# Value products of the plain, dilated and sparse heads in two column halves, with the probabilities weighted ahead

## The reference

```python
def hybrid_mixer(x, w_in, sinks, lam_p, sub_g, w_out, layer_idx, cos, sin):
    proj = jnp.einsum('bld,dk->blk', x, w_in)
    ...
    acc, m, l = banded_attention(qa, ka, va, SWA_WINDOW - 1)        # A: 8 heads, 2 key/value heads, a sink
    oa = (acc * (corr / den)[..., None]).reshape(b, A_HEADS, L, HEAD_DIM)
    ...
    ob = diff_attention(...)                                        # B: 4 heads, values 128 wide
    ob = ob * lax.rsqrt(jnp.mean(jnp.square(ob), -1, keepdims=True) + RMS_EPS) * sub_g * (1.0 - lam_init)
    oc = dilated_mixture(...)                                       # C: 8 heads
    od = dsa_attention(...)                                         # D: 8 heads, one value head, keys chosen
    mixed = jnp.concatenate([merge(oa), merge(ob), merge(oc), merge(od)], -1).astype(x.dtype)
    return jnp.einsum('blk,kd->bld', mixed, w_out)

def peer_ffn(x, wq, sub_keys, u, v):
    ...
        h = jnp.einsum('td,tkd->tk', xt, u[et])
        a = gt * jax.nn.gelu(h, approximate=False)
        return jnp.einsum('tk,tkd->td', a.astype(v.dtype), v[et])
```

## Time and profile before

| | us |
|---|---|
| median of 3 runs | 3949.77 (3948.16 to 3950.01) |
| the profiled execution's own time | 3949.41 |
| its span | 3947.6 |
| PE busy | 3889.0 (99%) |
| DVE busy | 2638.2 (67%) |
| ACT busy | 1980.8 (50%) |

### The profile page before, as it was taken

One profiled execution on the slowest core, in us unless ns is written; L12 is line 12 of the kernel. 1 busy time (PEld: TensorE's weight loads), 2 busy tenths in 40 slices (PEclk: granted clock), 3 DMA queues, 4 the chain that ended last, 5 costly groups with the idle time before them and its releaser, 6 DMA issues.

```text
span 3947.6 us, 63698 instructions
## 1 busy us (share of the span) xinstructions
PE 3889.0 (99%) x20356; PEld 3313.9 (84%) x20356; DVE 2638.2 (67%) x5016; ACT 1980.8 (50%) x2840; POOL 507.6 (13%) x716
## 2 busy tenths in 40 slices
PE   8999999999999999999999999999999999999998
PEld 6888888888898888888778878888888988888886
DVE  6765688658865555555677555886588655555556
ACT  4564545654565444444455544456555654444443
POOL 1100000730072000000011000017201710000000
PEclk9999999999999999999999999999999999999999
DMA  5435556559645666666644354654695456666664
GB/s 213 160 139 203 176 192 212 177 188 289 216 170 192 239 229 228 227 228 228 233 160 153 136 203 172 211 209 173 201 284 204 173 212 229 227 228 228 229 231 172
DMA packets 244174, 806.66 MB, mean 204 GB/s; under 512 B 24928, under 2 KB 157536, under 8 KB 159328
## 3 DMA queue, kind: packets, MB, share of 16 engines
q1 hardware_dynamic: 207200, 771.65, 56.2%
q10 hardware_dynamic: 36864, 33.57, 2.5%
HBM read 752.69 MB, written 52.43 MB: 204 GB/s over the span
## 4 chain that ended last, share of the span: by engine, by line
PE 96%; DVE 2%; ACT 1%; POOL 0%; DMA 0%; issue 0%; SPq 0%; ACTq 0%; DVEq 0%; POOLq 0%
PE bank L463 27%; PE bank L465 14%; PE bank L681 12%; PE bank L682 12%; PE bank L683 12%; PE bank L477 5%; PE bank L479 5%; PE bank L478 5%; PE bank L643 3%; PE bank L525 1%; PE bank L505 1%; PE bank L518 1%; PE bank L450 0%; DMA iota_k<-iota 0%; PE bank L620 0%; PE bank L490 0%
## 5 line engine op out<-in xcount | busy, mean ns | idle before, releaser
L1070 DVE TENSOR_TENSOR lo<-raw,hi 128x1024 fp32r<-128x1024 f32 x1312 | 1615.0, 1231 | 1015.0 <-ACT hi L730 967.8
L730 ACT ACTIVATE hi<-raw 128x1024 fp32r<-128x1024 f32 x1312 | 1388.6, 1059 | 1496.2 <-PE bank L683 756.9
L463 PE MATMUL bank<-xhl,hi 128*128 128x512 f32 x4608 | 1201.1, 396 | 3.6 <-DVE xhl L1086 2.2
L463 PEld LDWEIGHTS bank<-xhl,hi 128*128 128x128 f32 x4608 | 814.1, 189 | 136.8 <-DVE xhl L1086 2.8
L681 PE MATMUL bank<-hi,xhl 128*128 128x512 f32 x2048 | 797.8, 390 | 7.1 <-DVE xhl L1514 4.4
L682 PE MATMUL bank<-lo,xhl 128*128 128x512 f32 x2048 | 797.4, 389 | 0.0
L683 PE MATMUL bank<-hi,xhl 128*128 128x512 f32 x2048 | 797.2, 389 | 0.0
L465 PEld LDWEIGHTS bank<-xhl,lo 128*128 128x128 f32 x4608 | 655.7, 190 | 64.4
L465 PE MATMUL bank<-xhl,lo 128*128 128x256 f32 x4608 | 672.0, 282 | 0.0
L681 PEld LDWEIGHTS bank<-hi,xhl 128*128 128x128 f32 x2048 | 384.7, 188 | 88.1 <-DVE lo L1070 5.2
L683 PEld LDWEIGHTS bank<-hi,xhl 128*128 128x128 f32 x2048 | 384.9, 188 | 79.9
(11 more groups left out here) (149 smaller groups left out, 2229.3 us busy)
## 6 DMA issues: line engine op xcount, KB each, us to landing
raw<-u_t SPq DMA_DIRECT2D x256, 1024.0 KB, 5.0
raw<-v_t SPq DMA_DIRECT2D x256, 1024.0 KB, 4.8
raw<-w_in SPq DMA_DIRECT2D x80, 1024.0 KB, 4.8
raw<-w_out SPq DMA_DIRECT2D x32, 1024.0 KB, 4.8
raw<-wq SPq DMA_DIRECT2D x32, 1024.0 KB, 4.8
gelu_scratch<-gelu_out ACTq DMA_DIRECT2D x256, 128.0 KB, 3.1
scr<-gelu_scratch SPq DMA_DIRECT2D x256, 128.0 KB, 4.6
gates_scratch<-arena SPq DMA_DIRECT2D x32, 512.0 KB, 9.7
```

The costliest lines, as they stand in the source:

```text
L463: pe.matmul(acc[:], w, xhl[:, c, :, :].rearrange("p a t -> p (a t)"), start=(c == 0), stop=False)
L730: act.activation(hi[j % NSPLIT][:], half, ACT.Copy).then_inc(hi_done, 1)
L1070: dve.tensor_tensor(lo[j % NSPLIT][:], half, hi[j % NSPLIT][:].bitcast(F32), ALU.subtract).then_inc(lo_done, 1)
```

## The change

The value products of the heads of A, C and D are done for two heads at a time, in `pair_values`: now 64 columns of values are stationary and the 128 columns of the transposed probabilities are moving. The result of the first head goes to partitions 0 to 63 of the bank, that of the second to 64 to 127, so the result is already transposed (head elements on partitions, tokens along the row) and needs no turn of `mixed`. As the row sums would then lie along the row, the probabilities are divided ahead: ACT multiplies them by the inverted sums (`weigh`, two instructions for a head, in the slot after the exponentials), and `turn_probs` waits for that. `take_out` becomes a plain copy for A and D and nothing for C, whose result ACT and DVE split straight from the bank. Only the four heads of B still go through `mixed_b` and two turns (k = 4 and 5). Two more edits come with it: the wait for `iota_in` on DVE moves from the kernel's start to just before the expert selection, and the last products of each layer take, for token block 0, the half tiles one after another over all banks.

```diff
-    out = {t + 2: (e[0], e[1]) for t, e in slots.items() if e[0] in ("A", "D")}
+    out = {t + 2: (e[0], e[1] // 2) for t, e in slots.items() if e[0] in ("A", "D") and e[1] % 2}
@@ tensor
                     def turn_step(r, src, k):
-                        if r == 1 and k < 2:
-                            pe.wait_ge(v_stored, NB)
-                        elif r == 1 and k < 4:
+                        if r == 1:
                             pe.wait_ge(masked_done, NB * N_HEAD_ITEMS)
-                        elif r == 1:
-                            pe.wait_ge(turn_lo, n - 1)
+                            pe.wait_ge(rms_scaled, 4 * (k - 3))
...
-                            pe.wait_ge(exp_done, NB * (head_item(n) + 1))
+                            pe.wait_ge(weighted, NB * (WEIGHTED_NO[kind, h] + 1))
...
+                    def pair_values(dst, srcs, at):
+                        for b in range(NB):
+                            for kb in range(b + 1):
+                                for i in range(2):
+                                    last = pe.matmul(dst[i * HD:(i + 1) * HD, b * P:(b + 1) * P], vals[:, kb, at[i]:at[i] + HD],
+                                                     srcs[i][:, (b + kb) * P:(b + kb + 1) * P], start=(kb == 0), stop=(kb == b))
...
-                            for i in range(4):
-                                last = head_values(bank[7 - h][:, i * 2 * HD:(i + 1) * 2 * HD], probs_t_c[4 * h + i],
-                                                   V_C + HD * (4 * h + i), HD)
+                            for i in range(2):
+                                c = 4 * h + 2 * i
+                                last = pair_values(bank[7 - h][:, i * L:(i + 1) * L], probs_t_c[c:c + 2], [V_C + HD * c, V_C + HD * (c + 1)])
...
-                            last = head_values(bank[7], probs_t[j % 2], V_A + HD * (h // 4) if kind == "A" else V_D, HD)
+                            at = V_A + HD * (h // 2) if kind == "A" else V_D
+                            last = pair_values(bank[7], probs_t[2 * (j % 2):2 * (j % 2) + 2], [at, at])
...
-                        if t in MIXED_TURN_AT:
-                            turn_step(1, mixed, MIXED_TURN_AT.index(t))
+                        if t in MIXED_TURN_AT and MIXED_TURN_AT.index(t) in (4, 5):
+                            turn_step(1, mixed_b, MIXED_TURN_AT.index(t))
...
-                    for q in range(D // W):
-                        for j in (BODY - 4 + q // 2, BODY - 2 + q // 2):
-                            pe.wait_ge(lo_done, N_HALVES - BODY + j + 1)
-                            pe.wait_ge(al_done, NT - NRAW + j // 2 + 1)
-                            last = products(0, j, j // 2 % 2, stop=j >= BODY - 2, qs=(q % 2,))
-                        last.then_inc(y_done, 1)
+                    for j in range(BODY - 4, BODY):
+                        pe.wait_ge(lo_done, N_HALVES - BODY + j + 1)
+                        pe.wait_ge(al_done, NT - NRAW + j // 2 + 1)
+                        for q in range(2):
+                            last = products(0, j, j // 2 % 2, stop=j >= BODY - 2, qs=(q,))
+                            if j >= BODY - 2:
+                                last.then_inc(y_done, 1)
@@ scalar
+                        if r == 1 and k < 4:
+                            act.wait_ge(head_out, 2 * k + 2)
+                            act.wait_ge(half_used, AT_IN + N_IN - HPG + k + 1)
+                            act.activation(xh[:, 2 * k:2 * k + 2, :], mixed_t[:, 2 * k:2 * k + 2, :], ACT.Copy).then_inc(turn_hi, 1)
+                            return
...
+                    def weigh(n):
+                        kind, h, part = ITEMS[n]
+                        if kind == "B":
+                            return
+                        act.wait_ge(summed_up, WEIGHTED_NO[kind, h] + 1)
+                        for b in range(NB):
+                            i = NB * head_item(n) + b
+                            cols = pm[n % 4][:, block_cols[b]]
+                            act.activation(cols, cols, ACT.Identity, scale=st[:, 2, i:i + 1]).then_inc(weighted, 1)
...
+                        for n in ITEM_AT.get(t - 1, ()):
+                            if n >= N_INDEX:
+                                weigh(n)
@@ vector
                         dve.wait_ge(prepared, 4)
-                        dve.wait_ge(iota_in, 16)
...
+                        dve.tensor_copy(mixed_t[:, h + (4 if kind == "D" else 0), :], bank[7][:, 0:L]).then_inc(head_out, 1)
...
+                    dve.wait_ge(iota_in, 16)
                     for b in range(NB):
                         with dve.Fori(0, PH) as h:
```

More of the change, by code:

```diff
@@ L134, in build @@
     VALUE_AT, VALUE_NO = value_events()
-    N_SHORT = 2 * 8
+    N_TAKEN = 4 + 4 + len(B_VALUES_AT)
+    WEIGHTED_NO = {(kind, h): n for n, (kind, h, part) in enumerate(i for i in ITEMS if i[0] in ("A", "D", "C"))}
     ITEM_NO = {item: n for n, item in enumerate(ITEMS)}
@@ L191, in build @@
         ln2_gb, _ = region(16 * L, 2, D)
-        mixed, at = region(at, NB, D)
+        mixed_t, at = region(at, 8, L)
+        mixed_b, at = region(at, NB, W)
         bias_causal, at = region(at, L)
@@ L215, in build @@
         sel_flat = sel.rearrange("p a b n -> p (a b n)")
+        probs_t = [at[:, i * HEAD_COLS:(i + 1) * HEAD_COLS] for at in (scr[:, 1536:2304], sel_flat) for i in range(2)]
         probs_t_c = ([arena[:, h * HEAD_COLS:(h + 1) * HEAD_COLS] for h in range(2)]
@@ L254, in turn_bank @@
             if r == 1:
-                return bank[k] if k < 2 else bank[4 + k % 2]
+                return bank[13 - k] if k >= 6 else bank[4 + k % 2]
             return bank[4 + k % 4]
@@ L272, in build @@
         irelu, iacc = sem("irelu"), sem("iacc")
+        summed_up, weighted = sem("summed_up"), sem("weighted")
         scored, masked_done = sem("scored"), sem("masked_done")
@@ L447, in turn_step @@
                             pe.wait_ge(normed_dve, (2 if r and layer else 0) + k // 4 + 1)
+                        first_c = 8 if r == 1 else 0
                         for c in (2 * k, 2 * k + 1):
@@ L527, in head_values @@
                         return last
+                    def pair_values(dst, srcs, at):
[4 more added lines that the diff above has]
+                                                     srcs[i][:, (b + kb) * P:(b + kb + 1) * P], start=(kb == 0), stop=(kb == b))
+                        return last
                     def values(kind, h):
@@ L732, in turn_high @@
                     def turn_high(r, k):
-                        act.wait_ge(turned, r * (DC // 2) + k + 1)
+                        if r == 1 and k < 4:
[3 more added lines that the diff above has]
+                            return
+                        if r == 1 and k >= 6:
+                            act.wait_ge(pv_done, VALUE_NO["C", k - 6] + 1)
+                        else:
+                            act.wait_ge(turned, {0: k + 1, 1: DC // 2 + k - 3, 2: DC // 2 + 2 + k + 1}[r])
                         if r == 1:
@@ L1075, in turn_low @@
                         full = turn_bank(r, k)
-                        if r != 1 and k % 2 == 0:
+                        if r == 1 and k < 4:
+                            full = mixed_t[:, two, :].rearrange("p a b -> p (a b)")
+                        elif r != 1 and k % 2 == 0:
                             full = turn_f[0]
@@ L1322, in rms_scale @@
                             h, b = j // 2, j % 2
-                            cols = mixed[:, b, MIX_B + 2 * HD * h:MIX_B + 2 * HD * (h + 1)]
+                            cols = mixed_b[:, b, 2 * HD * h:2 * HD * (h + 1)]
                             dve.scalar_tensor_tensor(out=cols, in0=cols, scalar=small[:, 40 + j:41 + j], in1=subg_b, op0=ALU.mult,
```

45 lines of the change are left out of this document (13 added, 32 removed).

## The result

| | us |
|---|---|
| changed kernel, median of 6 runs | 3923.39 (3922.21 to 3924.08) |
| kernel before, median of 6 runs beside it | 3949.89 (3947.26 to 3950.64) |
| ratio | 0.9934, 95% interval 0.9922 to 0.9945 |
| profiled execution after: its own time, its span | 3923.11, 3921.3 |
| forecast | 3927, range 3920 to 3942 |

A forecast was written before the change was run, and what follows sets the result against it. PE, busy 3889.0 of 3947.6 us, was taken as the bound. Gains of 5.3 (turns), 8.2 (value products), 7.5 (start) and 1.7 (between layers) sum to 22.7 us: 3927 us, range 3920 to 3942.

The forecast's parts named there:

- What bounds the kernel: Whole kernel: PE is busy 3889.0 of 3947.6 us, so nearly every product removed from PE shortens it.
- Mixed turns: PE's turns of `mixed`: six go in each of two layers at 0.44 us each, 5.3 us gained.
- Value products: Value products of A, D and C in two column halves, two at a time: 8.2 us gained, bounds 14.2 and -7.6.
- The rival of one half after the other: Value products: column halves don't overlap, only 6.9 us gained in all, 3943 us; chance 16%.
- Weighting ahead: ACT's weighting of probabilities for 24 pairs of heads: costs PE 0, with a bound of 7 us.
- the tightest: Slots 76 and 77: ACT's weightings and store of C5 end 0.2 us before PE's turn of C6.
- The start: Kernel start without DVE's wait for `iota_k`: PE starts at 14.0, not 21.50; 7.5 us gained, bounds 5.5 and 7.5.
- The last products: End of each layer, twelve products ahead of the wait: 1.7 us gained between layers (bounds 0 and 2), 0 at the end.
- The sum: Whole kernel: 5.3 + 8.2 + 7.5 + 1.7 = 22.7 us gained, giving 3927 us.

The follow-up runs named there:

- both single experiments: The changed kernel with the old order of the last products, 3926.98 us; the kernel before with the new order alone, 3947.74 us against 3948.80 beside it.

## Why the prediction was right, point by point

**What bounds the kernel.** Right. PE is still busy for 99% of the span, and the turns and value products removed from it shortened their slots.

**Mixed turns.** 0.44 us for each was forecast; measured were 0.44, 0.45, 0.37, 0.47, 0.34, 0.47 and 0.11 at the slots concerned (the last is what a turn adds to the slot behind it), 2.64 a layer, 5.3 in all. The step holds to the tenth.

**Value products.** The mechanism was right, the size was not: 10.8 us in place of 8.2. The term that was mis-sized is what A and D gain, 2.1 us a layer forecast and 3.3 measured; C came as forecast (2.0 and 2.1). The forecast gave every head before 0.61 us and every pair after 0.96, "two at a time, plus 0.30 for going into that form and out of it". Two at a time is right (0.109 us for two passes of 128 columns), and the 0.30 isn't far off where split products stand ahead: by the prediction's own reckoning, from the product ahead plus 0.23, the pair in slot 33 takes 0.90 us (115.69 + 0.23 to 116.82), a price of 0.25. (The 0.16 above leaves out the 0.09 ahead of the group's first pass.)

What the sum lacked is that the price depends on what stands beside the group. Eight slots lose their head altogether; they became 5.0 us shorter in a layer, where 8 x 0.61 = 4.9 were forecast. Eight slots have a pair in place of one head, and should have become 8 x 0.35 = 2.8 us longer; they became 1.75 longer:

- By 0.12 to 0.14 us in slots 55, 57 and 62, where the pair stands behind scores. From the start of the last pass of the scores to what follows are 0.31 us, a pair in the changed kernel (191.550 to 191.856) or a head in the kernel before (196.205 to 196.511), so the pair pays for one change and not for two, and a head there had cost 0.72 and not 0.61.
- By 0.20 us in slots 33 and 41. The slot ahead of each lost its only small group, and the first split product behind a small group takes 0.31 us to the next one in place of 0.23, and that went too.
- By 0.29 to 0.34 us in slots 38, 46 and 65, nearly as forecast.

A rule was weighed in the prediction: by the Trainium skill, TensorEngine Tiling (Array Packing), Key Properties, a change of mode drains the engine and tiles work independently. The trace fits both: there is a price at each change, and it is paid once where two tiled groups follow each other. Of the loads of the value products, those of 64 stationary columns have 136 ns and those of 128 have 190. That is 54 ns less, as in the estimate from the Trainium skill's TensorE: Matmul & The Clock Gate, on LDWEIGHTS (0.05 us), but not half. Whether these 54 ns are part of what a pair costs was not separated.

**The rival of one half after the other** is excluded by the records of slot 33 and by the run with one column half: its 1.45 us from the first pass, 1.54 from the product ahead plus 0.23, are near what that rival had expected of a pair (1.6).

**Weighting ahead.** Forecast at 0, with a bound of 7; measured 0.3, in slot 73 alone. Four weightings take 1.48 us, the forecast had 1.6 to 1.8. Slot 77, called the tightest, showed no wait; the place that did is another one, slot 73, where PE takes the values of B between scores and turns: there ACT's copy of the values into `vals` (L795), which now stands behind four weightings, comes late.

**The start.** 7.5 forecast, 7.4 measured and 6.6 by putting the wait back. The place of the first product was right to 0.1 us. What the prediction says of the first half tile, 4.5 us of work at the lower clock as before, was not so: before, it took 5.3 us at a granted clock of 1.00, in the changed kernel 5.5 at 1.00, and 6.2 in its second profile at the lower clock. That 7.4 of the 7.5 us were left is thus in part luck of the execution; 6.8 were left in the second profile.

**The last products.** 1.7 between the layers was forecast, 1.8 measured, 1.7 in both single experiments; that the lower clock rather than the wait makes DVE wait for banks is what the kernel's end points to, where the same wait cost nothing in the one profile in which the clock stayed. At the end 0 is right for the two profiles compared; it should have been "0 or 1.7, as the clock goes".

**What was not in the sum.** About 1 us was gained at the second norm of layer 1, where no instruction was changed. Windows of the changed kernel there:

```profile
2326.00:2331.00 5.00, 3.65 (x16) 3.27 (x16) 1.91 (x5) 3.98 (x7) 0.00 (x0) 0.51 0.40 167
2331.00:2336.00 5.00, 4.95 (x26) 4.42 (x27) 4.00 (x7) 4.97 (x10) 0.00 (x0) 0.81 0.00 0
```

In the kernel before, the same work had 0.77 and then 0.55 in its two windows. The granted clock is low around PE's idle time in the norm, and where that stretch falls differs between executions: in its second profile the changed kernel takes 0.8 us less there than in its first, and so does the run without weighting. A difference of 1 us between two profiles is therefore not by itself to be put down to an edit; why this one arose is open.

**The sum.** So of the 3.6 us between the forecast's 22.7 and the 26.3 of the profiles, 2.6 are the value products, and 1.0 to 1.2 stand at the norm, where nothing was forecast. That the start came out within 0.1 us is better than this term repeats from one execution to the next.

## What to carry to other kernels

Small full precision products with 64 output columns left half of PE unused here: put two independent ones into the two column halves and issue them alternately. Here a pair cost 0.109 us for two passes, plus 0.16 once and 0.09 more behind split products, and it was cheapest behind a group that already stood in another form (the scores). Choose the orientation so that the result is already transposed, and pay for it on an engine with idle time, the scaling included. And look at the first instruction of each engine: a wait for data that is needed much later cost more here than all the turns of `mixed` that went, and postponing it was worth more than advancing its transfer.

## What the runs showed of the hardware

- A full precision pass with 64 or with 128 moving columns takes the same 0.109 us to the next one in these groups; with the second column half two of 128 columns fit into it.
- Products for the other column half begin beside earlier ones even from six places behind, at 0.27 us more for a pair than in alternating order.
- From the start of the last pass of a group in row halves to the next group are 0.31 us, whether that one stands in column halves or in none.
- A wait of PE of 2.2 us near the end was followed by a lower granted clock in two of three profiles (0.70 and 0.57, against 1.00), between the layers in all three (0.66, 0.61 and 0.64, over 5, 3 and 3 us). When it fell, it cost 1.4 to 1.7 us on DVE's chain; when it did not, nothing.
- Starting PE 1.2 to 1.6 us earlier gave a span of 3920.3 us in one profile and 3921.7 in the other, against 3921.0 and 3921.3 without: it can run ahead of the engines that feed it, stand still, and lose the clock.
